# High and low halves of weight slots and normed input as tiles of their own, each beginning at another byte of a 512-byte line

## The reference

```
x = x + 0.5 * swiglu(rms_norm(x, ffn1_norm), ffn1_wi, ffn1_wo)     # width 1408
c = split_cols(rms_norm(x, mix_norm) @ w_in + b_in)
y_sb, y_ml, y_mla = stick_breaking(c), mlstm(c), mla(c)
x = x + (g0*(y_sb@w_up_sb) + g1*(y_ml@w_up_ml) + g2*(y_mla@w_up_mla)) @ w_out
x = x + 0.5 * swiglu(rms_norm(x, ffn2_norm), ffn2_wi, ffn2_wo)
```

## Time and profile before

| | |
|---|---|
| median of 2 runs | 2482.38 us (2481.59 to 2483.16) |
| the profiled execution | 2479.0 us, span 2477.2 us |
| granted TensorE clock, mean | 0.994 of full |
| PE busy | 2429.3 us, 98% |
| POOL busy | 1316.0 us, 53% |
| DVE busy | 1218.6 us, 49% |
| ACT busy | 928.7 us, 37% |
| DMA | 213.37 MB, mean 86 GB/s |

### The profile page before, as it was taken

The page is one execution under the profiler, slowest core; times in us unless marked ns, Lnnn a source line. Parts: engine busy times, 40 slices in busy tenths (PEclk is TensorE's granted clock), DMA queues, the critical chain, the costliest instruction groups (busy, mean ns, idle before and its releaser), DMA issues. The chain is left out here.

```text
span 2477.2 us, 29028 instructions
## 1 busy us (share of the span) xinstructions
PE 2429.3 (98%) x11174; PEld 1945.5 (79%) x11174; DVE 1218.6 (49%) x1937; ACT 928.7 (37%) x1447; POOL 1316.0 (53%) x1593
## 2 busy tenths in 40 slices
PE   7999999999999999999999999999999999999999
PEld 7767778888888888777687888888887667788887
DVE  4787756423224432359734843333323796266331
ACT  4444443322223223453524432332325454344321
POOL 4654346656556555446245665555553562456554
PEclk9999999999999999999999999999999999999999
DMA  5211123333333333212122333333332221323332
GB/s 174 76 60 60 52 69 94 95 102 94 96 100 106 100 96 100 68 61 68 43 78 84 94 94 102 94 95 100 95 100 60 68 60 43 94 85 95 94 100 96
DMA packets 59609, 213.37 MB, mean 86 GB/s; under 512 B 6608, under 2 KB 6736, under 8 KB 59344
## 3 DMA queue, kind: packets, MB, share of 16 engines
q1 hardware_dynamic: 59472, 211.52, 27.9%
HBM read 209.39 MB, written 2.10 MB: 85 GB/s over the span
## 5 line engine op out<-in xcount | busy, mean ns | idle before, releaser
L664 PE MATMUL banks<-t,t 128*128 128x512 f32 (+5 forms) x10854 | 2398.7, 390 | 26.9 <-POOL t L1839 17.3
L664 PEld LDWEIGHTS banks<-t,t 128*128 128x128 f32 (+1 forms) x10854 | 1908.7, 189 | 489.4 <-issue 84.2
L1839 POOL TENSOR_TENSOR t<-t,t 128x256 fp32r<-128x256 f32 x1548 | 1263.0, 848 | 1126.9 <-ACT t L1576 1126.9
L1576 ACT ACTIVATE t<-t 128x1024 fp32r<-128x1024 f32 x387 | 410.2, 1060 | 1172.6 <-issue 607.2
L1118 DVE TENSOR_TENSOR t<-banks,t 128x512 f32<-128x512 f32 x121 | 83.4, 689 | 201.1 <-PE banks L664 200.7
L1282 DVE TENSOR_TENSOR t<-banks,t 128x512 f32<-128x512 f32 x44 | 30.4, 691 | 183.6 <-PE banks L664 183.5
L1250 DVE SCALAR_TENSOR_TENSOR t<-banks,t 128x512 f32<-128x512 f32 x32 | 22.1, 692 | 155.4 <-PE banks L664 155.4
L1006 DVE SCALAR_TENSOR_TENSOR t<-t,t,t 128x512 fp32r<-128x512 f32 x64 | 51.5, 805 | 61.7 <-ACT t L1585 61.7
L1227 DVE TENSOR_TENSOR t<-t,t 128x512 fp32r<-128x512 f32 x68 | 70.1, 1031 | 2.3
L1256 DVE TENSOR_TENSOR t<-banks,t 128x512 f32<-128x512 f32 x24 | 16.6, 692 | 106.0 <-PE banks L664 106.0
L1277 DVE TENSOR_TENSOR t<-banks,t 128x512 f32<-128x512 f32 x44 | 30.4, 692 | 70.3 <-PE banks L664 69.9
(11 more groups left out here) (160 smaller groups left out, 1239.2 us busy)
## 6 DMA issues: line engine op xcount, KB each, us to landing
t<-in_w SPq DMA_DIRECT2D x387, 512.0 KB, 3.5
t<-in_xT SPq DMA_DIRECT2D x8, 256.0 KB, 5.9
out<-t SPq DMA_DIRECT2D x8, 256.0 KB, 4.6
t<-in_dmask SPq DMA_DIRECT2D x1, 1536.0 KB, 11.9
t<-in_vbias SPq DMA_DIRECT2D x2, 384.0 KB, 3.9
t<-in_c SPq DMA_DIRECT2D x1, 576.0 KB, 8.5
t<-in_pos SPq DMA_DIRECT2D x2, 256.0 KB, 6.2
t<-in_smask SPq DMA_DIRECT2D x1, 256.0 KB, 12.1
```

The source lines that it names most:

```text
L664: return pe.matmul(o, l, r, start=start, stop=stop, skip_group_check=True)
L1576: a.activation(whl[u % 2][:, 0:1024], wraw[u % 3][:, :], ACT.Copy).then_inc(*w_high.next(u))
L1839: p.tensor_tensor(hl[:, 1024:2048][:, c], wraw[u % 3][:, c], as_f32(hl[:, c]), ALU.subtract).then_inc(*w_low.next((u, q)))
```

## The change

`whl` (two slots, each with its high and low half side by side) becomes four tiles, and `xs_t` becomes two, `xh_t` and `xl_t`. Ahead of each the allocator skips bytes until the tile begins at the byte of a 512-byte line that a table gives, and it does so again ahead of `tab`, from where all that follows begins at byte 128 as before. The tiles stand in the order w high 0, x low, w low 0, x high, w high 1, w low 1, each 64 bytes further in its line than the one ahead of it. All that follows them moves up by 512 bytes. `wraw` keeps byte 128.

In every engine's program the instructions, their shapes, their order and their semaphores stay as they were; only addresses differ.

```diff
+PHASE = {"w high 0": 192, "x low": 256, "w low 0": 320, "x high": 384, "w high 1": 448, "w low 1": 0, "tables": 128}
...
-        xs_t = take(16 * S, F32R)
-        XH = [xs_t[:, m * S:(m + 1) * S] for m in range(8)]
-        XL = [xs_t[:, (8 + m) * S:(9 + m) * S] for m in range(8)]
+        def phase(byte):
+
+            top[0] += (byte - base - top[0]) % 512
+
+        def operand(name, cols_):
+            phase(PHASE[name])
+            return take(cols_, F32R)
+
         wraw = [take(1024) for _ in range(3)]
-        whl = [take(2048, F32R) for _ in range(2)]
+        whigh, wlow = [operand("w high 0", 1024)], []
+        xl_t = operand("x low", 8 * S)
+        wlow.append(operand("w low 0", 1024))
+        xh_t = operand("x high", 8 * S)
+        whigh.append(operand("w high 1", 1024))
+        wlow.append(operand("w low 1", 1024))
+        XH = [xh_t[:, m * S:(m + 1) * S] for m in range(8)]
+        XL = [xl_t[:, m * S:(m + 1) * S] for m in range(8)]
+        phase(PHASE["tables"])
         tab = take(2 * S)
...
             def weights(n):
                 u, i = divmod(n, 8)
-                hl = whl[u % 2]
                 need.wait_ge(*w_low.at((u, i // 2)))
-                return hl[:, 128 * i:128 * i + 128], hl[:, 1024 + 128 * i:1152 + 128 * i]
+                return whigh[u % 2][:, 128 * i:128 * i + 128], wlow[u % 2][:, 128 * i:128 * i + 128]
...
-                rh = whl[u % 2][:, 128 * i:128 * (i + n)]
-                rl = whl[u % 2][:, 1024 + 128 * i:1024 + 128 * (i + n)]
+                rh = whigh[u % 2][:, 128 * i:128 * (i + n)]
+                rl = wlow[u % 2][:, 128 * i:128 * (i + n)]
...
-                a.activation(whl[u % 2][:, 0:1024], wraw[u % 3][:, :], ACT.Copy).then_inc(*w_high.next(u))
+                a.activation(whigh[u % 2][:, :], wraw[u % 3][:, :], ACT.Copy).then_inc(*w_high.next(u))
...
-                hl = whl[u % 2]
                 for q in range(4):
                     c = slice(256 * q, 256 * q + 256)
-                    p.tensor_tensor(hl[:, 1024:2048][:, c], wraw[u % 3][:, c], as_f32(hl[:, c]),
+                    p.tensor_tensor(wlow[u % 2][:, c], wraw[u % 3][:, c], as_f32(whigh[u % 2][:, c]),
                                     ALU.subtract).then_inc(*w_low.next((u, q)))
```

## The result

| | before | after |
|---|---|---|
| median | 2482.38 us | 2519.23 us (2519.21 to 2519.25, 2 runs) |
| profiled execution | 2479.0 us, span 2477.2 | 2519.2 us, span 2517.4 |
| ratio | | 1.0148 (95% interval 1.0105 to 1.0192) |

The change makes the kernel 37 us slower, 1.5%. The forecast was 2481 us and no change. The time lies in the forecast range, and within the 2% of its middle class, but the interval leaves "no change" out.

What follows compares the result with a forecast made beforehand. PE was taken as the bound, by matmul count times start-to-start distance (226.8 ns). All terms were put at 0, summing to 0 us against the profiled 2479.0 us: forecast 2481 us, no change, 8-in-10 range 2395 to 2560 us.

Steps and rivals of the forecast that it cites:

- middle class: Whole kernel: time within 2% (50 us) of no change, chance 0.52.
- What bounds the kernel: PE, with a matmul 98% of the span: time is matmul count by start-to-start distance, 226.8 ns for 512 columns.
- Instructions, waits, ACT, POOL, the loads: cost 0: All engines' programs: nothing added or moved, ACT's and POOL's new operand bytes harmless, 387 loads land as before; 0 us.
- PE's operands: cost 0: 9072 F32R matmuls: new start bytes leave the pace unchanged, 0 us, bounded by 115 us off and 112 us on top.
- the strided rows' 12 ns: 96 matmuls reading weights at every fourth column: 239 ns pace, 12 ns more; upper bound of 112 us if all paid it.
- The faster rival: PE's load and stream clash because they start at equal bytes; 2366 us, or 2424 with half the excess gone; chance 0.27.
- The slower rival: Equal bytes are lucky; loads 64 to 384 bytes ahead hold PE's stream; 2593 us, or 2537 at half; chance 0.21.
- 268 or fewer: PE records in the stretch 682 to 744 us that would show slowing; 274 or 275 meant no change.
- pace differs between slots: PE's pace differing from one 24 matmuls to the next would show that distance in the line matters; no size given.
- Little of either: PE's gains at some distances and losses at others cancel within 2%: 2440 to 2525 us, chance 0.10.
- The plain float32 rows: PE's plain float32 matmuls: 214.5 ns per 512 columns, 1.2 over the columns, so they don't pay the F32R excess.
- The lower bound of the sum: F32R matmuls all reaching the plain float32 pace: 12.3 ns by 9072, with 288 shorter ones, 115 us off.

Runs made afterwards that it cites:

- the sweep: PE-only program, not the kernel: each segment fixes how many bytes further the load begins than the stream (distance); 226.7 ns at 0, up to 234.3 ns at 96.
- the two sequences alone: PE-only segments, not the kernel, repeating the changed kernel's bytes for normed-input streams with weight slot 0 or 1: 233.3 and 231.05 ns.

## Why the prediction was wrong

- **What bounds the kernel** was right: the time followed PE's distance from start to start and nothing else. 4.9 ns by 9072 are the 44 us by which PE's busy time grew.
- **Instructions, waits, ACT, POOL, the loads: cost 0** was right. 188, 840 and 1061 ns stayed, and the split alone is 0.9996.
- **PE's operands: cost 0** is the step that failed, in its link "if the excess came from loads and streams asking for the same part of a memory, ACT, DVE, POOL and the DMAs should disturb the pace too". The reading under it stands: in the two windows after, too, PE passes 269 and 268 records with DVE busy 15.94 and 24.62 us. The inference doesn't. PE's stream and PE's load disturb each other although the other engines leave no mark on the pace, and the sweep shows it with all others idle. The prediction named this link as the likeliest to break, and gave the slower side 0.21; it had no row of F32R at another contiguous distance, and the strided rows' 12 ns were the sign that a load's pattern moves the pace. They were set aside as a longer load. The measured cost of this term is 4.9 ns a matmul, 44 us of PE's busy time, in place of 0.
- **The faster rival** falls: distance 0 is not the cause of the excess but the best place of all that ran. The forecast's own reading, "a fixed price of an F32R matmul's change of weights, which no address touches", does not hold either: addresses add up to 7.7 ns to it, and the 13.3 ns at distance 0, the same for 256, 384 and 512 columns, are 15.6 to 22.5 at lengths between 448 and 504.
- **The slower rival** had the right sign, "today's equal bytes are the lucky ones", and its count, "268 or fewer" in 682 to 744 us, was missed by one record, 269. Its mechanism, a pursuit that lasts until the load ends and grows to 94 ns, has little support: the price does not grow with the distance, and a load of a quarter of the length lowers it by 2 to 3 ns at distances 64 and 128 and raises it by 5 at 0. Its two sizes, 12 and 6 ns, were both too large; the dearest place of the sweep is 7.7 ns over, and the change's mixture averages 4.9, just under the 5.5 from which it would have decided.
- **The sign "pace differs between slots"** is there: streams of the normed input go at 233.2 ns a matmul with slot 0 and 231.3 with slot 1, from the starts in the trace; the two sequences alone gave 233.3 and 231.05.
- **"Little of either"** has the time, 2519 in its 2440 to 2525 us, and not the reason: it has gains and losses that cancel, and no place in the sweep gains. That the time fell inside the forecast range as well is because the cost is small, not because a step of the argument foresaw it.
- **The plain float32 rows** were read as 1.2 ns over 512 columns "though every one has its load". There is one load to 0.429 us, so the excess beside one load is 429.2 - 426.7 = 2.5 ns. The lower bound of the sum would have been 10.9 ns a matmul, some 102 us off, and not 115; the forecast does not hang on it.

The Trainium skill, TensorE: Matmul & The Clock Gate, section "Step-by-step: what each phase is for", has two independent read ports, so that a load takes nothing from the running matmul. For F32R that does not hold to the nanosecond: with nothing changed but where the load begins, the stream's pace went from 226.7 to 234.3 ns.

What stays open: what in PE makes them meet, why several paces hold for one sequence once bytes change, and where the 13.3 ns at distance 0 come from. No pattern of 512 columns that ran goes under them, so no version faster than the kernel before came out of this.

## What to carry to other kernels

Let the loads and the streams of back-to-back F32R matmuls all begin at one and the same byte modulo 256: pairs that matched each other but changed from matmul to matmul went 1.4 to 2% slower here, behind slower segments. Tiles that are multiples of 256 bytes long, laid one after the other, do that by themselves, and by the sweep an odd small tile ahead of one operand costs up to 3.4% of the time of such matmuls. That other engines leave the pace alone says nothing about an engine's own two readers: a program with that engine alone and one byte varied per segment settles it in a single run. And before concluding from such a sweep, run one sequence after different preambles, since the pace can depend on what ran before.

## What the runs showed of the hardware

- F32R matmuls, 512 columns, one load of 128 each: with unvarying bytes 226.67 ns from start to start at a distance of 0 or 16 bytes either way, modulo 256, and 228.8 to 234.3 at the other multiples of 16. A load begun 4, 8 or 12 bytes off is worse than one 16 off: 232.5, 230.7 and 229.8 ns.
- Each load at the byte of the stream beside it, but the byte changing by 128 from one matmul to the next or in turns of three, behind slower segments: 229.9 and 231.1 ns.
- The same 72 matmuls at 228.9, 231.1 or 233.2 ns by what ran before them.
- A stream of 504 columns takes as long as one of 512 (226.67 ns); 496 take 223.3, and 488 more than that, 225.9.
- Plain float32 of 512 columns: two records a matmul, 429.2 ns each, at distances 0, 32, 64, 128 and 192 alike.
